# Padding a token tile, splitting the gather around a transpose, and re-laying the experts' weights in a hybrid GLA/GDN + MoE step on one Trainium2 core

## Chip, core and metric

The kernel runs on one NeuronCore of a Trainium2 chip. The metric is device time in microseconds, from the first to the last instruction of one launch. The engines are TensorE (PE, with its weight loads shown apart as PEld), VectorE (DVE), ScalarE (ACT), GpSimd (POOL) and SyncE (SP), which here issues all DMAs.

## What is computed

One decoder layer for 256 prompt tokens and 8 sequences of 4 sample tokens (288 tokens, width 1024): adaLN modulation, a mixer with a GLA and a Gated DeltaNet branch, an output projection, and then a hierarchical mixture of experts, which is the part that the change touches. All arithmetic is float32.

```python
def _moe(h, w_gr, b_gr, w_er, b_er, w_g, w_u, w_d):
    ...
    comb = ((one_hot(g_idx[:, 0], N_GROUPS) * g_w)[:, :, None] * within[:, None, :])
    for g in range(N_GROUPS):                       # 4 groups of 4 experts
        a = jnp.einsum('md,edf->mef', hf, w_g[g])   # D = 1024 -> F = 512
        u = jnp.einsum('md,edf->mef', hf, w_u[g])
        hid = jax.nn.silu(a) * u * comb[:, g, :, None]
        out = out + jnp.einsum('mef,efd->md', hid, w_d[g])
```

Each token goes to two of the sixteen experts (the top two of one group). An expert's three matrices are 1024 x 512, 1024 x 512 and 512 x 1024, 2 MB each.

## The kernel before

The program first runs the adaLN products, the input projections and the two mixer branches, with weights in a ring of five buffers (`W`, 1 MB each), then the output projection (`wout`), the second norm, the router, the experts, and the final norm. It is written by hand, one function per engine, with semaphores between engines.

**Router.** On PE, `token_major(m)` (L959) transposes the normed hidden state from feature-major (`hT`) to token-major, in three token tiles, `TILES = ((0, 128), (128, 128), (256, 32))`: two of 128 tokens and one of 32. ACT copies each half tile of 512 features from PSUM into `h2t` (L2211). DVE runs a chain of some forty small operations that picks groups and experts, and takes two exponentials from ACT on the way (L2221, L2224). POOL clears some tables and the accumulator `acc` (L2332 to L2337).

**Experts.** Eight blocks of two experts each. An expert has 64 token slots, a pair 128. DVE writes the one-hot matrix `Dg` (token x slot) of the pair and its weighted copy `Dc` in `dispatch` (L1815, L1818). The work of a block on PE (`expert_block`, L1004) is, in its order:

1. gate products, 16 matmuls (8 steps over the features, two experts, 64 output columns of the array each, 512 wide), into PSUM bank 2;
2. three transposes of `Dc` into bank 4 (L1025);
3. up products, 16 matmuls, into bank 3;
4. `gather` of the next block (L993): for each of 8 chunks of 128 features, three matmuls, one per token tile, that add up to the features of the 128 slots. The third one has a weight of 32 rows only, `h2t[0:32]`, since the last token tile has 32 tokens. Chunks 0 to 3 go to bank 0, 4 to 7 to bank 1;
5. four transposes of `hid` (L1035), after a wait for DVE, which makes `hid` = up x silu(gate) (L1843);
6. down products, 16 matmuls, after a wait for DVE, which copies the transposed `hid` from PSUM to `hidT` (L1847);
7. eight scatter products (L1050) of 288 columns each, which DVE adds to `acc` (L1854).

Each matmul in float32 is two passes on PE, so the profile counts 48 for the 24 matmuls of a gather. All of PE's products stand under the helper's line L431, transposes under L434. The gathered features of the next block are read by DVE (`gather_read`, L1827, bank 0) and ACT (L2229, bank 1). The last block has no gather. Blocks 0 to 5 are written as a loop of two, so that the gate weights of odd blocks lie in a buffer of their own (`gate2`). Experts with over 64 tokens would take a further loop (`overflow`, L474); in the profiled execution it ran no block.

**Weights.** SP loads a pair's gate, up and down weights, 4 MB each, with one DMA each (`load_expert`, L2427). Feature k x 128 + p goes to partition p, chunk k, so that each partition gets 16 runs of 2 KB for gate and for up, and 8 runs of 4 KB for down. The loads of a pair wait for PE's products of the pair before (L2449 to L2454): gate weights one block ahead (two buffers), up and down weights as soon as their one buffer is free.

Of the kernel before, what the change touches and what calls it, by code (L numbers as in the profile page):

```python
# [18 lines left out]
ALU = mybir.AluOpType  # L19
ACT = mybir.ActivationFunctionType  # L20
AX = mybir.AxisListType.X

P = 128
D = 1024
KD = D // P
# [3 lines left out]
TILES = ((0, 128), (128, 128), (256, 32))  # L29
# [28 lines left out]
PAIR = 2 * SLOTS  # L58
# [58 lines left out]
class Signals:  # L117
# [15 lines left out]
    def mark(self, kind, *events, by=1):  # L133
        sem = self.sem(kind)
        self.value[kind] += by
        for event in events:
            assert event not in self.marks, event
            self.marks[event] = (kind, self.value[kind])
        return sem

    def when(self, event):
        kind, value = ("first_building", 1) if self.counts is None else self.counts[event]
        return self.sem(kind), value
# [9 lines left out]
def _program(nc, ctx, I, O, known):  # L153
    S = Signals(nc, ctx, known)
    mark, when = S.mark, S.when
# [131 lines left out]
    h2t = carve(3, D)  # L287
    acc = carve(KD, TOK)
    Dg, Dc = carve(3, 2, SLOTS), carve(3, 2, SLOTS)
    DT_ = carve(TOK)  # L290
    hg = carve(KD, PAIR)
    hid = carve(DE)
# [24 lines left out]
    pm = [ctx.enter_context(nc.psum_tensor(f"bank{i}", [P, 512], F32)) for i in range(8)]  # L317

    T, V, A, G = nc.tensor, nc.vector, nc.scalar, nc.gpsimd
# [67 lines left out]
    for item in schedule:  # L387
        kind, c = item[0], item[-1]
# [38 lines left out]
    def rb(name):  # L427
        return pm[banks.get(name, 0)]
# [4 lines left out]
    def tr(out, in_, n):  # L433
        return T.transpose(out, in_, ident[0:n, 0:n])  # L434
# [53 lines left out]
    def _(pe):  # L488
# [501 lines left out]
            mm(b[0:q, 0:1], tri[0:q, 0:q], over[0:q, 0:1])  # L990
            mm(b[0:1, 8:9], over[0:q, 0:1], ones[0:q, 0:1]).then_inc(mark("router_products", "over ready"), 1)

        def gather(i, n):  # L993

            pe.wait_ge(n["dispatch"], i + 1)
            for g in range(2):
                for k in range(4):
                    for m, (o, w) in enumerate(TILES):
                        last = mm(pm[g][:, PAIR * k:PAIR * k + PAIR],
                                  h2t[0:w, m, 512 * g + 128 * k:512 * g + 128 * k + 128],  # L1000
                                  Dg[0:w, m].rearrange("p a b -> p (a b)"), m == 0, m == 2)
                last.then_inc(n["gathered"], 1)

        def expert_block(i, n, loaded_sem, second, gates, gates_loaded, more):  # L1004

            def products(out, lhs, kind, k, half, K):
                for x in range(2):
                    wt = (EW[:, kind] if kind else gates)[:, x * second, :].rearrange("p (k n) -> p k n", k=K)  # L1010
                    last = mm(out[SLOTS * x:SLOTS * x + SLOTS, :], lhs[:, k, SLOTS * x:SLOTS * x + SLOTS],
                              wt[:, k, 512 * half:512 * half + 512], k == 0, k == K - 1)
                return last

            pe.wait_ge(*gates_loaded)
            pe.wait_ge(n["gather_read0"], i + 1)
            for k in range(KD):
                if k == 4:
                    pe.wait_ge(n["gather_read1"], i + 1)
                last = products(pm[2], hg, 0, k, 0, KD)  # L1020
            last.then_inc(n["gate"], 1)

            pe.wait_ge(n["added"], KD * i + 1)
            for m, (o, w) in enumerate(TILES):
                last = tr(pm[4][0:PAIR, o:o + w], Dc[0:w, m].rearrange("p a b -> p (a b)"), w)  # L1025
            last.then_inc(n["scatter_matrix"], 1)
            pe.wait_ge(loaded_sem[1], 16 * (i + 1))
            for k in range(KD):
                last = products(pm[3], hg, 1, k, 0, KD)
            last.then_inc(n["up"], 1)  # L1030
            if more:
                gather(i + 1, n)
            pe.wait_ge(n["hidden"], i + 1)
            for f in range(4):
                last = tr(pm[5][:, PAIR * f:PAIR * f + PAIR], hid[0:PAIR, 128 * f:128 * f + 128], PAIR)  # L1035
            last.then_inc(n["turned"], 1)
            pe.wait_ge(loaded_sem[2], 16 * (i + 1))
            pe.wait_ge(n["turned_read"], i + 1)
            for g in range(2):
                for k in range(4):  # L1040
                    last = products(pm[6 + g], hidT, 2, k, g, 4)
                last.then_inc(n["down"], 1)
            pe.wait_ge(n["down_read0"], i + 1)
            for d in range(KD):

                if d == 3:
                    pe.wait_ge(n["down_read1"], i + 1)
                if d >= 4:
                    pe.wait_ge(n["added"], KD * i + d - 2)
                last = mm(pm[4 + d % 4][:, 0:TOK], yt[0:PAIR, 128 * d:128 * d + 128], DT_[0:PAIR, :])  # L1050
                last.then_inc(n["scattered"], 1)
# [44 lines left out]
    def _(dve):  # L1096
# [733 lines left out]
        def expert_block(i, n, next_dispatch):  # L1830

            s = sg2[0:PAIR]
            dve.wait_ge(n["softplus"], i + 1)
            V.scalar_tensor_tensor(s, pm[2][0:PAIR, :], 0.0, s, ALU.min, ALU.subtract).then_inc(n["log_sigmoid"], 1)  # L1834
            dve.wait_ge(n["scatter_matrix"], i + 1)
            V.tensor_copy(DT_[0:PAIR, :], pm[4][0:PAIR, 0:TOK]).then_inc(n["scatter_matrix_read"], 1)
            dve.wait_ge(n["sigmoid"], i + 1)
            V.tensor_tensor(s, pm[2][0:PAIR, :], s, ALU.mult).then_inc(n["silu"], 1)
            if next_dispatch:
                next_dispatch()  # L1840
            dve.wait_ge(n["silu"], i + 1)
            dve.wait_ge(n["up"], i + 1)
            V.tensor_tensor(hid[0:PAIR], pm[3][0:PAIR, :], s, ALU.mult).then_inc(n["hidden"], 1)  # L1843
            if next_dispatch:
                gather_read(i + 1, n)
            dve.wait_ge(n["turned"], i + 1)
            V.tensor_copy(hidT, pm[5][:, 0:4 * PAIR].rearrange("p (k s) -> p k s", s=PAIR)) \  # L1847
                .then_inc(n["turned_read"], 1)
            dve.wait_ge(n["down"], 2 * i + 1)
            V.tensor_copy(yt[0:PAIR, 0:512], pm[6][0:PAIR, :]).then_inc(n["down_read0"], 1)  # L1850
            dve.wait_ge(n["added"], KD * i + 1)
            for d in range(KD):
                dve.wait_ge(n["scattered"], KD * i + d + 1)
                V.tensor_tensor(acc[:, d, :], acc[:, d, :], pm[4 + d % 4][:, 0:TOK], ALU.add).then_inc(n["added"], 1)  # L1854
# [75 lines left out]
    def _(act):  # L1930
# [275 lines left out]
        def router():  # L2206
            def token_major(m):
                n = TILES[m][1]
                for g in range(2):
                    act.wait_ge(*when(f"h2t{m}{g} ready"))  # L2210
                    A.activation(h2t[0:n, m, 512 * g:512 * g + 512], rb(f"h2t{m}{g}")[0:n, :], ACT.Copy) \  # L2211
                        .then_inc(mark("router_by_scalar", f"read h2t{m}{g}"), 1)

            act.wait_ge(*when("router parts ready"))
            for i in range(4):
                act.wait_ge(*when(f"stored {chunk_of[('sgdn', i)]}"))
            A.activation(rparts, rb("router parts")[:, 0:TOK], ACT.Copy) \
                .then_inc(mark("router_by_scalar", "read router parts"), 1)
            token_major(0)
            act.wait_ge(*when("gd"))  # L2220
            A.activation(rs_["dd"], rs_["dd"], ACT.Exp).then_inc(mark("router_by_scalar", "gexp"), 1)  # L2221
            token_major(1)
            act.wait_ge(*when("ed"))
            A.activation(rs_["p1"], rs_["p1"], ACT.Exp).then_inc(mark("router_by_scalar", "eexp"), 1)  # L2224
            token_major(2)

        def gather_read(i, n):
# [49 lines left out]
    def _(pool):  # L2277
# [48 lines left out]
        def router():  # L2326

            pool.wait_ge(*when("merged 7"))
            pool.wait_ge(*when("wout7 ready"))
            for i in range(4):  # L2330
                pool.wait_ge(*when(f"stored {chunk_of[('sgdn', i)]}"))
            G.memset(rank, 0.0)  # L2332
            G.memset(comb, 0.0)
            G.memset(rt, 0.0).then_inc(mark("cleared", "rt zero"), 1)

            G.memset(acc, 0.0).then_inc(main_sems["added"], 1)
            G.memset(combJ, 0.0).then_inc(over_sems["added"], 1)  # L2337
# [5 lines left out]
    def _(sp):  # L2343
# [83 lines left out]
        def load_expert(kind, experts, n, sems, into=None):  # L2427

            sem = gate2_loaded if into is gate2 else sems[kind]
            into = EW[:, kind] if into is None else into  # L2430
            sp.dma_start(into[:, 0:n, :].rearrange("p a (k n) -> p (a k) n", k=4 if kind == 2 else KD),
                         wts[kind][experts].rearrange("a (k p) n -> p (a k) n", p=P)).then_inc(sem, 16)


        sp.wait_ge(*when("gdn2 oT1"))
# [87 lines left out]
```

## Time and profile before

| | before |
|---|---|
| median of 3 runs | 963.03 us (962.93 to 964.56) |
| profiled execution: its own time | 962.34 us |
| its span, first to last instruction | 960.4 us |
| PE busy | 876.6 us, 91% of the span |
| DVE, ACT, POOL busy | 399.9, 258.2, 35.2 us |
| moved by DMA | 190.65 MB, 199 GB/s over the span |
| expert blocks (first gather to the last scatter) | about 644 to 940 us |

The page gives shares of an average; the order of reading is: the forty slices for where the stages lie, the chain of work that ended last for what sets the end in a stage, then the timeline of one turn of the loop there. "PEclk" is the granted TensorE clock, 1.0 being 2.4 GHz and 0.5 being 1.2 GHz. A matmul's duration in the trace is its latency, so its rate is read from the starts of a stretch, not from the mean.

### The profile page before, as it was taken

How to read it: one execution, taken by the hardware profiler on the slowest of the kernel's cores; microseconds unless marked ns; L12 is line 12 of the kernel's file. 1: busy time of each engine (PE TensorE's matmuls, PEld its weight loads, DVE VectorE, ACT ScalarE, POOL GpSimd, SP SyncE). 2: the span in 40 equal slices, each digit the busy share in tenths (PEclk: the TensorE clock that was granted, in tenths of full speed). 3: DMA queues.
4: the chain of work that ended last, by engine and by line, in shares of the span. 5: the costliest groups of instructions: out<-in, count | busy, mean ns of one | idle time of the engine just before them, and what ended most of it. 6: DMA issues, size and time to landing. Idle time of an engine off the chain costs nothing.

```text
span 960.4 us, 12485 instructions
## 1 busy us (share of the span) xinstructions
PE 876.6 (91%) x4791; PEld 594.3 (62%) x4791; DVE 399.9 (42%) x992; ACT 258.2 (27%) x626; POOL 35.2 (4%) x84
## 2 busy tenths in 40 slices
PE   5889999898898899999999978779999999999995
PEld 3557777666666798879887736555544544544533
DVE  3120004656687855664555384341222222222216
ACT  3121103665554333434335320121011011011012
POOL 0000000000400000000001003000000000000000
PEclk9969999999998999999999957957999999999998
DMA  8947666522557321222216318991999998997621
GB/s 206 347 142 228 205 222 213 177 89 88 172 179 240 113 87 45 88 88 69 65 44 170 108 48 246 326 387 50 349 375 338 347 377 331 354 363 265 254 96 51
DMA packets 134412, 190.65 MB, mean 199 GB/s; under 512 B 6656, under 2 KB 90283, under 8 KB 134309
## 3 DMA queue, kind: packets, MB, share of 16 engines
q1 hardware_dynamic: 134360, 189.94, 58.7%
q8 instruction: 35, 0.57, 0.2%
q14 instruction: 17, 0.14, 0.1%
HBM read 178.98 MB, written 10.95 MB: 198 GB/s over the span
## 4 chain that ended last, share of the span: by engine, by line
PE 80%; DVE 10%; ACT 4%; issue 2%; SPq 2%; DMA 1%; DVEq 0%; POOL 0%; ACTq 0%; POOLq 0%
PE bank L431 78%; PE bank L434 3%; DVE arena L1693 2%; DMA arena<-in_w_ada 1%; DVE arena L1271 1%; DVE arena L1847 1%; DVE arena L1134 1%; ACT arena L1945 1%; SPq L2365 0%; ACT arena L1938 0%; DVE arena L1256 0%; ACT arena L1936 0%; ACT arena L1949 0%; DVE arena L1571 0%; ACT arena L2042 0%
## 5 line engine op out<-in xcount | busy, mean ns | idle before, releaser
L431 PE MATMUL bank<-arena 128*128 128x288 f32 (+8 forms) x4494 | 834.9, 414 | 60.4 <-DVE arena L1158 8.6
L431 PEld LDWEIGHTS bank<-arena 128*128 128x128 f32 (+4 forms) x4494 | 559.0, 174 | 322.2 <-issue 178.2
L434 PE MATMUL bank<-arena 128*128 128x128 f32 (+6 forms) x297 | 50.3, 302 | 18.7 <-DMA arena<-in_w_conv 7.3
L434 PEld LDWEIGHTS bank<-arena 128*128 128x128 f32 (+6 forms) x297 | 35.8, 154 | 38.9 <-issue 19.5
L2042 ACT ACTIVATE arena<-arena 128x288 f32<-128x288 f32 (+1 forms) x56 | 25.1, 448 | 122.0 <-DVE arena L1256 122.0
L1854 DVE TENSOR_TENSOR arena<-arena,bank 128x288 f32<-128x288 f32 x64 | 28.8, 455 | 29.4 <-PE bank L431 28.0
L1271 DVE SCALAR_TENSOR_TENSOR arena<-arena 128x312 f32<-128x312 f32 x72 | 39.4, 547 | 2.5
L1834 DVE SCALAR_TENSOR_TENSOR arena<-bank,arena 128x512 f32<-128x512 f32 x8 | 5.5, 692 | 77.2 <-ACT arena L2239 77.2
L1125 DVE TENSOR_TENSOR arena<-bank,arena 128x18 f32<-128x18 f32 x24 | 4.2, 174 | 77.9 <-PE bank L431 77.9
L2229 ACT ACTIVATE arena<-bank 128x512 f32<-128x512 f32 x8 | 4.8, 598 | 111.7 <-PE bank L431 111.7
L1940 ACT ACTIVATE arena<-arena 128x288 f32<-128x288 f32 (+4 forms) x60 | 33.5, 558 | 2.0
L2075 ACT ACTIVATE arena<-bank 128x288 f32<-128x288 f32 x40 | 16.2, 405 | 53.9 <-PE bank L431 30.2
L1256 DVE SCALAR_TENSOR_TENSOR arena<-arena 128x288 f32<-128x288 f32 (+1 forms) x56 | 25.9, 463 | 8.7 <-ACT arena L1940 8.7
L1434 DVE TENSOR_TENSOR arena<-arena 128x512 f32<-128x512 f32 x28 | 18.9, 690 | 23.0 <-PE bank L431 23.0
L1938 ACT ACTIVATE arena<-arena 128x288 f32<-128x288 f32 (+4 forms) x60 | 28.0, 466 | 1.9
L1504 DVE TENSOR_TENSOR arena<-arena,bank 128x512 f32<-128x512 f32 x24 | 16.5, 689 | 26.6 <-PE bank L431 26.6
L1936 ACT ACTIVATE arena<-arena 128x288 f32<-128x288 f32 (+2 forms) x57 | 25.5, 448 | 4.9 <-DMA arena<-in_cc 4.1
L2235 ACT ACTIVATE arena<-bank 128x512 f32<-128x512 f32 x8 | 4.8, 597 | 81.1 <-PE bank L431 81.1
L2245 ACT ACTIVATE arena<-bank 128x512 f32<-128x512 f32 x8 | 4.8, 598 | 71.0 <-PE bank L431 71.0
L1945 ACT ACTIVATE arena<-bank,arena 128x288 f32<-128x288 f32 x19 | 9.5, 500 | 48.7 <-PE bank L431 48.7
L1850 DVE COPY arena<-bank 128x512 f32<-128x512 f32 x8 | 5.5, 691 | 32.4 <-PE bank L431 32.4
L1827 DVE COPY arena<-bank 128x512 f32<-128x512 f32 x8 | 5.5, 692 | 31.1 <-PE bank L431 31.1
(238 smaller groups left out, 441.4 us busy)
## 6 DMA issues: line engine op xcount, KB each, us to landing
arena<-in_w_in SPq DMA_DIRECT2D x36, 1024.0 KB, 6.8
arena<-in_w_exp_gate SPq DMA_DIRECT2D x8, 4096.0 KB, 13.9
arena<-in_w_exp_up SPq DMA_DIRECT2D x8, 4096.0 KB, 17.1
arena<-in_w_exp_down SPq DMA_DIRECT2D x8, 4096.0 KB, 13.0
arena<-in_w_ada SPq DMA_DIRECT2D x24, 1024.0 KB, 5.6
arena<-in_state_gla SPq DMA_DIRECT2D x4, 1024.0 KB, 6.9
out_gla_s<-arena SPq DMA_DIRECT2D x4, 1024.0 KB, 8.9
arena<-in_w_out SPq DMA_DIRECT2D x4, 1024.0 KB, 6.1
```

The costliest lines, as they stand in the source:

```text
L431: return T.matmul(out, lhsT, rhs, start=start, stop=stop)
L434: return T.transpose(out, in_, ident[0:n, 0:n])
L1256: V.scalar_tensor_tensor(sg, y, 0.0, sg, ALU.min, ALU.subtract) \
L1271: V.scalar_tensor_tensor(y, x[:, j:j + YW], wv(j), y, ALU.mult, ALU.add) \
L1434: V.tensor_tensor(Lm[0:n, hs, 0:n], LT[0:n, hs, 0:n], mid(const(f"level{lv}")[0:n, 0:n], HG), ALU.mult) \
L1693: last = V.scalar_tensor_tensor(st, st, eSs[:, s, h:h + 1], pm[4 + j][:, P * q:P * q + P], ALU.mult, ALU.add)
L1854: V.tensor_tensor(acc[:, d, :], acc[:, d, :], pm[4 + d % 4][:, 0:TOK], ALU.add).then_inc(n["added"], 1)
L1936: A.activation(dst, src, ACT.Abs).then_inc(mark(kind, event + " abs"), 1)
L1938: A.activation(dst, dst, ACT.Exp, scale=-1.0).then_inc(mark(kind, event + " exp"), 1)
L1940: A.activation(dst, dst, ACT.Ln, bias=one[0:n]).then_inc(mark(kind, event), 1)
L1945: A.activation(dst, src, ACT.Ln, bias=const("eps")[0:n], scale=scale) \
L2042: A.activation(sg, sg, ACT.Exp).then_inc(mark("proj_by_scalar", f"sig{s3}"), 1)
```

## The change

Four edits. (a) The third token tile of `h2t` is cleared over all 128 partitions by POOL, ACT waits for that before it writes the 32 tokens, and the gather's third matmul takes 128 rows like the other two. (b) The gather of the next block is split: its first half (bank 0) stays where it was, its second half (bank 1) stands behind the four transposes of `hid`. (c) The weights of an expert are loaded so that partition p holds the features p x 8 + k (gate, up) and p x 4 + k (down), which lie side by side in memory: one run of 16 KB for each partition and expert. (d) To match, ACT writes `h2t` with its features permuted, with a step of 512 bytes between the elements it writes one after the other, and DVE makes `hid` from operands that it reads with a step of 16 bytes.

```diff
-        def gather(i, n):
+        def gather(i, n, halves=(0, 1)):
 
             pe.wait_ge(n["dispatch"], i + 1)
-            for g in range(2):
+            for g in halves:
                 for k in range(4):
-                    for m, (o, w) in enumerate(TILES):
+                    for m in range(3):
                         last = mm(pm[g][:, PAIR * k:PAIR * k + PAIR],
-                                  h2t[0:w, m, 512 * g + 128 * k:512 * g + 128 * k + 128],
-                                  Dg[0:w, m].rearrange("p a b -> p (a b)"), m == 0, m == 2)
+                                  h2t[:, m, 512 * g + 128 * k:512 * g + 128 * k + 128],
+                                  Dg[:, m].rearrange("p a b -> p (a b)"), m == 0, m == 2)
                 last.then_inc(n["gathered"], 1)
...
             if more:
-                gather(i + 1, n)
+                gather(i + 1, n, (0,))
             pe.wait_ge(n["hidden"], i + 1)
             for f in range(4):
                 last = tr(pm[5][:, PAIR * f:PAIR * f + PAIR], hid[0:PAIR, 128 * f:128 * f + 128], PAIR)
             last.then_inc(n["turned"], 1)
+            if more:
+                gather(i + 1, n, (1,))
...
-            V.tensor_tensor(hid[0:PAIR], pm[3][0:PAIR, :], s, ALU.mult).then_inc(n["hidden"], 1)
+
+            V.tensor_tensor(hid[0:PAIR].rearrange("s (k p) -> s k p", k=4),
+                            pm[3][0:PAIR, :].rearrange("s (p k) -> s k p", k=4),
+                            s.rearrange("s (p k) -> s k p", k=4), ALU.mult).then_inc(n["hidden"], 1)
...
-                    A.activation(h2t[0:n, m, 512 * g:512 * g + 512], rb(f"h2t{m}{g}")[0:n, :], ACT.Copy) \
+
+                    A.activation(h2t[0:n, m, :].rearrange("t (k c a) -> t c a k", k=KD, c=KD)[:, 4 * g:4 * g + 4],
+                                 rb(f"h2t{m}{g}")[0:n, :].rearrange("t (c a k) -> t c a k", c=4, k=KD), ACT.Copy) \
...
             A.activation(rs_["p1"], rs_["p1"], ACT.Exp).then_inc(mark("router_by_scalar", "eexp"), 1)
+            act.wait_ge(*when("h2t padding"))
             token_major(2)
...
             G.memset(rt, 0.0).then_inc(mark("cleared", "rt zero"), 1)
+            G.memset(h2t[:, 2, :], 0.0).then_inc(mark("cleared", "h2t padding"), 1)
...
-            sp.dma_start(into[:, 0:n, :].rearrange("p a (k n) -> p (a k) n", k=4 if kind == 2 else KD),
-                         wts[kind][experts].rearrange("a (k p) n -> p (a k) n", p=P)).then_inc(sem, 16)
+
+            sp.dma_start(into[:, 0:n, :], wts[kind][experts].rearrange("a (p k) n -> p a (k n)", p=P)) \
+                .then_inc(sem, 16)
```

On PE, in the loop of the experts, from the up products to the down products (the difference; in brackets the semaphores that an instruction waits for, `expert_hidden` being DVE's product L1843 and `expert_turned_read` its copy L1847):

```order
 L431 MATMUL bank<-arena 128x128 [waits expert_dispatch]
-L431 MATMUL bank<-arena 128x128 x23
+L431 MATMUL bank<-arena 128x128 x11
 L434 MATMUL bank<-arena 128x128 [waits expert_hidden]
 L434 MATMUL bank<-arena 128x128 x3
+L431 MATMUL bank<-arena 128x128 [waits expert_dispatch]
+L431 MATMUL bank<-arena 128x128 x11
 L431 MATMUL bank<-arena 64x512 [waits expert_turned_read,expert_loaded2]
```

Twelve of the gather's matmuls now stand between the transposes and the down products, which wait for DVE's copy.

On SP, the three loads of a pair in the loop, before and now (partitions x runs x elements):

```order
L2431 DMA arena<-in_w_exp_gate 128x16x512
L2431 ISA [waits expert_up]
L2431 DMA arena<-in_w_exp_up 128x16x512
L2431 DMA arena<-in_w_exp_down 128x8x1024 [waits expert_down]
```

```order
L2441 DMA arena<-in_w_exp_gate 128x2x4096
L2441 ISA [waits expert_up]
L2441 DMA arena<-in_w_exp_up 128x2x4096
L2441 DMA arena<-in_w_exp_down 128x2x4096 [waits expert_down]
```

Order and waits are the same; 16 or 8 runs in a partition have become 2 of 4096 elements.

## Rows read from the trace of the kernel before

**Rows 1.** The page, forty slices of 24 us: granted clock and DMA share, in tenths.
```profile
PEclk9969999999998999999999957957999999999998
DMA  8947666522557321222216318991999998997621
```

**Rows 2.** Chain that ended last, one loop turn, later the last block (start us, us, what).
```profile
719.42 0.70 DVE arena L1847
...
720.26 18.20 PE bank L431 x80
...
739.00 15.47 PE bank L431 x80
...
755.10 0.70 DVE arena L1847
...
924.52 0.70 DVE arena L1843
```

**Rows 3.** Timeline of that turn, weight loads (start us, us, [idle before <-releaser]).
```profile
745.96 8.32 PEld L431 LDWEIGHTS bank<-arena 128*128 128x128 f32 x48 [0.81 <-issue]
754.40 0.42 PEld L434 LDWEIGHTS bank<-arena 128*128 128x128 f32 x4
755.91 0.23 PEld L431 LDWEIGHTS bank<-arena 128*64 128x64 f32 x4 [1.08 <-issue]
```

**Rows 4.** Stretches, PEld alone: stretch, us, busy (count), clock, DMA share, GB/s.
```profile
745.96:754.40 8.44, 6.51 (x48) 1.00 1.03 386
497.89:503.25 5.36, 5.36 (x49) 1.00 0.00 0
```

**Rows 5.** Groups by form in the stretch 497.89 to 503.25 (count | busy us, mean ns).
```profile
L431 PEld LDWEIGHTS bank<-arena 128*128 128x128 f32 x49 | 5.6, 192 | 0.1
```

**Rows 6.** Timeline of that turn, VectorE, and SyncE's issue of the up weights.
```profile
746.15 0.69 DVE L1843 TENSOR_TENSOR arena<-bank,arena 128x512 f32<-128x512 f32 x1 [2.34 <-PE bank L431]
750.29 0.69 DVE L1827 COPY arena<-bank 128x512 f32<-128x512 f32 x1 [3.45 <-PE bank L431]
...
746.21 0.37 SPq L2431 DMA_DIRECT2D arena<-in_w_exp_up  x1
```

**Rows 7.** Stretches, PE alone: wout's start, first gather, first gate products.
```profile
579.95:586.00 6.05, 6.05 (x13) 0.50 0.71 210
586.00:618.00 32.00, 32.00 (x133) 1.00 0.86 282
644.00:658.97 14.97, 14.97 (x49) 0.50 0.27 99
658.97:661.09 2.12, 2.12 (x7) 0.50 0.00 0
```

**Rows 8.** Timeline of the router: ScalarE and VectorE.
```profile
631.92 1.07 ACT L2211 ACTIVATE arena<-bank 128x512 f32<-128x512 f32 x2
634.46 0.21 ACT L2224 ACTIVATE arena<-arena 128x12 f32<-128x12 f32 x1 [1.48 <-DVE arena L1778]
...
632.53 0.21 DVE L1775 TENSOR_TENSOR arena<-arena 128x48 f32<-128x48 f32 x1
632.77 0.23 DVE L1776 TENSOR_REDUCE arena<-arena 128x12 f32<-128x48 f32 x1
```

**Rows 9.** Timeline of the router: GpSimd's clearing of the accumulator.
```profile
614.79 2.02 POOL L2336 MEMSET arena<- 128x2304 f32 x1
```

**Rows 10.** Stretches, all engines: 4 KB runs, 2 KB runs, 12 KB runs among others.
```profile
731.00:738.00 7.00, 7.00 (x34) 2.18 (x32) 0.89 (x2) 0.00 (x0) 0.00 (x0) 1.00 1.02 412
741.00:762.00 21.00, 20.12 (x105) 10.85 (x103) 5.09 (x9) 1.23 (x2) 0.00 (x0) 1.00 1.03 385
...
8.00:11.00 3.00, 0.03 (x1) 0.03 (x1) 1.21 (x1) 1.69 (x3) 0.03 (x1) 1.00 1.21 237
```

**Rows 11.** DMA issues: KB each, median us to landing.
```profile
arena<-in_w_ada SPq DMA_DIRECT2D x24, 1024.0 KB, 5.6
...
arena<-in_const SPq DMA_DIRECT2D x1, 936.0 KB, 4.9
```

## Prediction

> **What bounds the kernel now.** I read the page first. Its slices show a granted clock of 1.0 nearly throughout the last third, and DMA busy to nine tenths there [rows 1]: the experts' stage could be bound by TensorE or by its weights. The chain of waits decides that. In the loop each turn takes 755.10 - 719.42 = 35.68 us, and all of it is PE but 0.70 us of VectorE's copy of the turned `hid` and its hand-over [rows 2]. No piece of the chain there is a DMA. So TensorE sets the pace, and only what shortens PE's own sequence counts. The timeline of the turn's weight loads then shows the two places that the edits touch: the gather's 48 passes, and the pause before the down products [rows 3].
>
> **Padding, edit (a).** The gather takes 754.40 - 745.96 = 8.44 us for 48 passes [rows 3, 4], 0.176 us each. The Gated DeltaNet branch has a stretch of passes with the same shape, all 128 rows high: 49 weight loads start within 5.36 us at the same clock [rows 4], 48 intervals of 0.1117 us. The present gather differs in its third matmul alone, 32 rows high, so that TensorE changes its tile size twice in each chunk. With all passes 128 high I take the stream's rate: 48 x 0.1117 = 5.36 us, which saves 3.08 us a turn. POOL's clearing of 1024 columns costs about 2.02 x 1024 / 2304 = 0.9 us [rows 9]. It starts at about 615 us, and its reader, ACT's third token tile, comes behind the exponential at 634.46 [rows 8], so it is hidden. If that cover were gone, 0.9 us would be added once.
>
> A rule speaks against this edit. The Trainium skill, TensorE: Matmul & The Clock Gate, Part 3 (The mechanism), says that a weight load overlaps running matmuls only where its row group differs from theirs. By that rule a column of full-height passes would hide no load and the padding would gain nothing. The trace disagrees: 49 loads of 192 ns each [rows 5] would need 9.4 us one after the other, and stood in 5.36 us.
>
> **Split, edit (b).** From the first load of the four transposes to that of the down products are now 755.91 - 754.40 = 1.51 us [rows 3], mostly the wait for DVE. With 12 matmuls behind the transposes, these cost four passes, 0.45 us, and PE goes on. For the change to 64-column tiles at the second half's end I add 0.10 us, an estimate between nothing and 0.19 us, what each of the 16 changes of tile size in a gather comes to (3.08 / 16). That saves 1.51 - 0.55 = 0.96 us a turn. The cover must hold: from the start of the gather's first half, at T = 0, the half lasts 2.7 us, DVE's product is ready at about 0.9 (it starts 0.2 after the last up product and takes 0.69) [rows 6], and the transposes end at 3.2. DVE reads the first half from 2.8 to 3.5, then copies the turned `hid` until about 4.3. PE reaches the down products at 5.9. So the wait has 1.6 us to spare, and the product 1.8 us.
>
> **Strided operands, edit (d).** DVE's product reads with a step of 16 bytes. The nearest row is a reduction that reads 48 elements with that step: 0.23 us against 0.21 for an operation on 48 contiguous ones [rows 8]. Scaled to 512 elements that is 0.2 us, upper bound twice its time, 0.7 us, lower bound nothing. In seven turns the 1.8 us cover it; in the last block, which has no gather, it lies in the chain [rows 2]. ACT's six copies to `h2t` write with a step of 512 bytes; no row shows such writes. The pair of 1.07 us has 1.48 us of slack before the second exponential [rows 8]. Up to 2.4 times their present time nothing moves; at four times the router's chain would be about 2 us late. I take nothing for both, since the nearest row shows almost nothing, and keep 0 to 2.7 us for the range.
>
> **Weights, edit (c).** Nothing waits for them now, so their layout is worth nothing by itself. But a turn shrinks to 35.68 - 3.08 - 0.96 = 31.64 us, and its three loads of 4.19 MB, 12.58 MB in that time, are 398 GB/s, where 2 KB runs moved 385 and 4 KB runs 412 GB/s while they streamed [rows 10]. Longer runs moved faster in every pair I can form: 1 MB in 1 KB runs landed 5.6 us after its issue, and 936 KB in runs of 7.5 KB 4.9 us after [rows 11]. I take 412 GB/s or more for runs of 16 KB, as the nearest row. Then the three loads of a turn take 30.5 us and keep up. What if they do not is rival B.
>
> **The first gather** is made at the low clock: 14.97 us, and the clock came up only 2.12 us into the gate products [rows 7]. A full-height pass at half the clock is twice 0.1117, so 48 take 10.7 us, a saving of 4.3. But it may also raise the clock earlier: wout's dense stream raised it 6.05 us after it began [rows 7], while today's gather, a third of whose passes change the tile size, did not in 14.97 us. I assume that it rises 5 us into the gather: 22.4 passes by then, the other 25.6 in 2.9 us, 7.9 us in all, a saving of 7.1; and the 2.12 us of gate products at half speed become 1.06. Together 8.1, with bounds of 4.3 (no rise before the gate products) and 9.1 (a rise after 3 us).
>
> **The sum.** Seven turns have a gather behind their up products: 7 x (3.08 + 0.96) = 28.3 us. With 8.1 for the first gather: 36.4 us. The profiled execution took 962.34 us, so 925.9; the median of the runs stands 0.7 above it, so 926.6 us. By the lower bound of the first gather and the upper ones of the strided operands it would be 933, by the best ends 924 to 925.
>
> **Rivals.**
> - **B, the weights become the bound.** Up weights have one buffer, so block 7's up load can only follow those before it. In the new schedule the first gate products start at 651.9, the first load of the loop is issued behind them at 658.9 and flows from about 661, and block 7 wants its up weights at 651.9 + 7 x 31.64 + 7.6 = 881. Nineteen loads of 4.19 MB lie in these 220 us, 79.7 MB: the bound begins below 362 GB/s, pauses included. Today's mean is 12.58 MB in 35.68 us, 353 GB/s, but with a pause in each turn, since loads wait for buffers. If 353 were all that the queue can give, block 7's up weights would come 226 - 220 = 6 us late and its down weights some 2.5 more: 935 us. For it: DMA share of nine tenths already [rows 1]. Against it: 385 and 412 GB/s while streaming [rows 10]. The Trainium skill, DMA: Bandwidth & Descriptors, Specifications, puts the limit of HBM for one core at about 358 GB/s; by that the loads would be 3 us late and the time 931 to 932. The trace disagrees already, with 412 GB/s over 7 us [rows 10].
> - **C, long runs are slow, and the kernel is slower than before.** One place has long runs: the convolution state, 24 partitions with 12 KB each, falls into a stretch that moved 237 GB/s [rows 10]. If 16 KB runs held the queue to 300 GB/s, the nineteen loads would take 266 us, 46 late, the last down load 5 more: 977 us. It decides below about 314 GB/s, where 34 us of lateness and some 2.5 of the last load eat the gain. Against it: that stretch is the program's start, with many small loads, and 24 partitions are few; the constants, 7.5 KB in all 128, were the quickest [rows 11].
> - **D, the padding gains nothing**, because a gather's pass waits for something else than its height, such as the alternation of weights. Then only the split is left, 7 x 0.96 = 6.7 us: 956.3. Against it: the stream at 0.1117 us also has a new weight for each pass, 49 loads [rows 4, 5]. The skill's rule cited under edit (a) would end here too.
>
> **How the numbers follow.** The forecast has 0.82: its terms come from rows of the same shape, and what is unsure is the first gather. B has 0.10, D 0.05, C 0.03. The range must leave out no more than 2 in 10: from 921, a little under the best ends, to 938, which takes in the strided operands and most of B. Left out are D, C, the rest of B and what is faster still, some 0.15. A measurement of this kernel can tell 0.2%, about 2 us, from no change. A, B and D are all faster by more: 0.96 with a rest for the unforeseen; C gives slower, 0.03, and 0.01 is left for no change.
>
> **What would show it.** In the profile after, the turn of the loop should be 31.6 us; the gather's two halves 2.7 us each, with no idle PE before the down products; the clock at 1.0 before the first gather ends; the first gate products at about 652 us. If PE waits in the loop for `in_w_exp_up`, it is B or C, and the loads' time to landing tells which. If the halves still take 4.2 us each, it is D. If VectorE's product takes over 2.5 us, the split's cover is gone and the transposes wait. The prediction is wrong if the turn is above 33 us, or if the router's chain has grown by over 3 us.

## Result and profile after

| | before | changed |
|---|---|---|
| median of the runs made side by side | 962.98 us (961.65 to 964.56) | 924.14 us (922.52 to 924.96) |
| ratio | | 0.9594, 95% interval 0.9574 to 0.9614 |
| profiled execution: time, span | 962.34, 960.4 us | 924.96, 923.1 us |

The change is 4.1% faster; forecast were 926.6 us, in a range from 921 to 938. In the profiled executions the difference is 962.34 - 924.96 = 37.4 us, of a sum of 36.4 forecast.

The page's forty slices after the change, granted clock and DMA share, answer to [rows 1]:

```profile
span 923.1 us, 12487 instructions
...
PEclk9969999999999899999999995896999999999998
DMA  8955765543267711233111632797499999997711
```

The slices of the last third look as before; what changed shows in the chain. The chain of work that ended last, one turn of the loop, the first piece of the next, then the last block (start us, us, what), answers to [rows 2]:

```profile
668.25 20.79 PE bank L431 x104
689.04 0.55 PE bank L434 x3
689.58 9.91 PE bank L431 x56
699.49 0.44 PE bank L434 x4
699.93 20.81 PE bank L431 x104
...
886.88 1.06 DVE arena L1846
...
888.68 0.70 DVE arena L1852
```

A turn is 699.93 - 668.25 = 31.68 us, and VectorE has left it: the piece of 104 passes runs from the gather's second half through the down and scatter products into the next gate products without a break. Only the last block, which has no gather, still waits for VectorE twice, and the product there has grown from 0.70 [rows 2] to 1.06 us.

The timeline of TensorE's weight loads in one turn (start us, us, [idle before <-releaser]) answers to [rows 3]:

```profile
728.24 2.75 PEld L431 LDWEIGHTS bank<-arena 128*128 128x128 f32 x24 [0.81 <-issue]
730.92 0.47 PEld L434 LDWEIGHTS bank<-arena 128*128 128x128 f32 x4
731.36 3.08 PEld L431 LDWEIGHTS bank<-arena 128*128 128x128 f32 x28
```

The first half starts at 728.24 and the transposes at 730.92: 2.68 us for 24 passes, 0.1117 each, which is the rate of the Gated DeltaNet stream [rows 4] to the digit. The second half follows the transposes by 0.44 us; its row of 28 runs on into the first four loads of the down products. Before, the down products followed the transposes by 1.51 us [rows 3], most of it a wait.

Stretches of the changed kernel: of all engines, with stretch, us, then busy time and count of PE, PEld, DVE, ACT and POOL, granted clock, DMA share and GB/s. The first two lie in the first gather, the third is one turn, the fourth a load of down weights, the last nearly the whole loop:

```profile
644.00:647.50 3.50, 3.50 (x19) 3.50 (x18) 0.00 (x0) 0.00 (x0) 0.00 (x0) 0.50 0.00 0
647.50:651.00 3.50, 3.50 (x28) 2.97 (x29) 0.69 (x1) 0.60 (x1) 0.00 (x0) 0.97 0.00 0
700.00:731.00 31.00, 31.00 (x163) 15.00 (x162) 8.96 (x17) 3.78 (x6) 0.00 (x0) 1.00 0.97 395
734.00:741.00 7.00, 7.00 (x35) 2.30 (x34) 0.69 (x1) 0.60 (x1) 0.00 (x0) 1.00 1.01 433
662.00:840.00 178.00, 178.00 (x948) 90.33 (x945) 53.42 (x96) 20.07 (x32) 0.00 (x0) 1.00 0.97 398
```

The clock rises inside the first gather, at about 647.7 us, 5.6 us after it began at 642.1; before, it stayed at half through all of it [rows 7]. In the loop PE is busy for 178 us of 178, at the full clock, while the queue moves 398 GB/s at a share of 0.97.

Timelines of VectorE, ScalarE and GpSimd (start us, us, [idle before <-releaser]): the product that makes `hid`, the copies to `h2t`, the second exponential, and the clearing of the padded tile, answer to [rows 6, 8]:

```profile
728.43 1.07 DVE L1846 TENSOR_TENSOR arena<-bank,arena 128x512 f32<-128x512 f32 x1 [2.34 <-PE bank L431]
...
629.88 1.89 ACT L2217 ACTIVATE arena<-bank 128x512 f32<-128x512 f32 x2
...
632.43 0.21 ACT L2231 ACTIVATE arena<-arena 128x12 f32<-128x12 f32 x1 [0.66 <-DVE arena L1780]
...
612.97 0.95 POOL L2343 MEMSET arena<- 128x1024 f32 x1
```

Strides cost something after all: the product takes 1.07 us where it took 0.69, and a pair of overlapping copies 1.89 where it took 1.07 [rows 8]. Both are covered: the product's 1.07 us lie under a half gather of 2.68, and ScalarE's slack before the exponential shrinks from 1.48 to 0.66 us but does not end. VectorE's chain of the router, from L1740 to the last weight, takes 8.40 us in both traces.

### The profile page after: what moved, and what is told of

It is laid out like the page before. It is cut to its first block, busy times and chain, and to the rows that moved or that the text cites. A ratio compares the mean times of both kernels' runs of the same rounds, so it can differ in the third digit from the quotient of the medians.

```text
span 923.1 us, 12487 instructions
## 1 busy us (share of the span) xinstructions
PE 843.6 (91%) x4791; PEld 578.1 (63%) x4791; DVE 402.5 (44%) x992; ACT 260.6 (28%) x626; POOL 36.1 (4%) x85
## 4 chain that ended last, share of the span: by engine, by line
PE 80%; DVE 10%; ACT 4%; issue 2%; SPq 2%; DMA 1%; POOL 0%; DVEq 0%; ACTq 0%; POOLq 0%
PE bank L431 78%; PE bank L434 3%; DVE arena L1695 2%; DMA arena<-in_w_ada 1%; DVE arena L1273 1%; DVE arena L1136 1%; ACT arena L1950 1%; SPq L2374 1%; POOL arena L2331 0%; ACT arena L1943 0%; DVE arena L1258 0%; ACT arena L1941 0%; ACT arena L1954 0%; DVE arena L1573 0%; DVE arena L1468 0%
## 5 line engine op out<-in xcount | busy, mean ns | idle before, releaser
L431 PE MATMUL bank<-arena 128*128 128x288 f32 (+8 forms) x4494 | 806.0, 409 | 55.7 <-DVE arena L1160 8.6
L431 PEld LDWEIGHTS bank<-arena 128*128 128x128 f32 (+4 forms) x4494 | 544.5, 174 | 301.8 <-issue 168.5
L434 PE MATMUL bank<-arena 128*128 128x128 f32 (+6 forms) x297 | 48.0, 291 | 19.2 <-DMA arena<-in_w_conv 7.6
L1855 DVE COPY arena<-bank 128x512 f32<-128x512 f32 x8 | 5.5, 691 | 43.5 <-PE bank L431 43.5
L1982 ACT ACTIVATE arena<-arena 128x288 f32<-128x288 f32 x8 | 3.5, 443 | 50.9 <-DVE arena L1731 50.9
```

The lines of the kernel that those rows point to most:

```text
L431: return T.matmul(out, lhsT, rhs, start=start, stop=stop)
```

## Experiments

Line numbers are those of each kernel. The median of before differs a little between comparisons, so ratios are given.

**Padding alone (`pad_only`).** Edit (a) without the others.

```diff
-                    for m, (o, w) in enumerate(TILES):
+                    for m in range(3):
...
-                                  h2t[0:w, m, 512 * g + 128 * k:512 * g + 128 * k + 128],
-                                  Dg[0:w, m].rearrange("p a b -> p (a b)"), m == 0, m == 2)
+                                  h2t[:, m, 512 * g + 128 * k:512 * g + 128 * k + 128],
+                                  Dg[:, m].rearrange("p a b -> p (a b)"), m == 0, m == 2)
...
+            act.wait_ge(*when("h2t padding"))
...
+            G.memset(h2t[:, 2, :], 0.0).then_inc(mark("cleared", "h2t padding"), 1)
```

> Edit (a) alone on the kernel before. Theory (a pass of the gather costs 0.112 us once all passes are 128 rows high, because the tile size no longer changes): the gather falls from 8.44 to 5.4 us, the turn from 35.68 to 32.6 us, the first gather and its gate products save about 7.7 us: 963.0 - 7 x 3.08 - 7.7 = 933.7 us. Rival (the padding gains nothing without the other edits, or the weights at 2 and 4 KB runs hold up a turn under 35 us): 945 to 963 us, with PE waiting for the weights.

Measured: 928.88 us (928.18 to 930.46), ratio 0.9656, interval 0.9638 to 0.9673. The chain, one turn:

```profile
703.17 0.70 DVE arena L1847
704.01 18.20 PE bank L431 x80
...
722.76 12.59 PE bank L431 x80
735.35 0.45 PE bank L434 x4
735.82 0.70 DVE arena L1847
```

The turn is 735.82 - 703.17 = 32.65 us, 3.03 less than 35.68, as forecast; 2.88 of it lie in the piece with the gather (15.47 to 12.59), the rest in the transposes behind it (0.60 to 0.45). The first gather and gate products, one piece of 84 passes, went from 24.07 to 16.41 us in the chain, 7.7 less. Seven turns and this piece make 28.9; the whole is 33.4 us in the spans (960.4 to 927.0). Of the other 4.5 us, 2.5 lie ahead of the first gather (its piece starts at 640.52 us instead of 643.03) and 0.3 behind the last scatter, in code that the edit does not touch. The last 1.7 lie in the down and scatter products of the last block, whose code is the same too, before and here:

```profile
926.80 12.88 PE bank L431 x48
895.38 11.18 PE bank L431 x48
```

The granted clock made that difference: 0.57 in the first 3.7 us of this piece before (926.80 to 930.50), 1.00 in the same place here (895.38 to 898.90). The changed kernel's trace has 12.88 us there too, so these 1.7 us are no part of its gain.

**Split alone (`split_only`).** Edit (b) without the others.

```diff
-                gather(i + 1, n)
+                gather(i + 1, n, (0,))
...
+            if more:
+                gather(i + 1, n, (1,))
```

> Edit (b) alone. Theory (PE's pause before the down products is the wait for VectorE's copy, and half a gather covers it): 0.96 us a turn in seven turns, 956.3 us; the first gather as before, 15.0 us. Rival (the pause is the change of tile size at the start of the down products, not the wait): nothing, 963 us.

Measured: 948.9 us (945.83 to 953.18), ratio 0.9855, interval 0.983 to 0.988. The chain:

```profile
700.38 11.26 PE bank L431 x56
711.63 0.59 PE bank L434 x4
712.22 22.15 PE bank L431 x104
...
746.17 0.59 PE bank L434 x4
746.76 22.14 PE bank L431 x104
```

The turn is 746.76 - 712.22 = 34.54 us: 1.14 less, where 0.96 were forecast. Together the two edits save 4.00 in a turn, so behind the padding the split is worth 32.65 - 31.68 = 0.97, as forecast. That it is worth 0.17 more alone, about one change of tile size, agrees with the order of passes: there the gather's last change, out of a 32-row tile, also leads to the 64-column tiles of the down products, which in the padded gather are a change more. This is argued from the order and was not tried by itself. Seven turns make 8 us. Between the profiled spans are 9.1 (960.4 to 951.3), but stretches outside the loop enter into that with up to 3 us either way: the first gather's piece starts 3.1 us earlier and takes 1.3 longer (25.36 against 24.07). The median is 14 below that of before, among runs that spread over 7 us. What goes beyond the loop's 8 us is not shown to be the split's.

**Layout alone (`runs_only`).** Edits (c) and (d) without the others.

```diff
-            V.tensor_tensor(hid[0:PAIR], pm[3][0:PAIR, :], s, ALU.mult).then_inc(n["hidden"], 1)
+            V.tensor_tensor(hid[0:PAIR].rearrange("s (k p) -> s k p", k=4),
+                            pm[3][0:PAIR, :].rearrange("s (p k) -> s k p", k=4),
+                            s.rearrange("s (p k) -> s k p", k=4), ALU.mult).then_inc(n["hidden"], 1)
...
-                    A.activation(h2t[0:n, m, 512 * g:512 * g + 512], rb(f"h2t{m}{g}")[0:n, :], ACT.Copy) \
+                    A.activation(h2t[0:n, m, :].rearrange("t (k c a) -> t c a k", k=KD, c=KD)[:, 4 * g:4 * g + 4],
+                                 rb(f"h2t{m}{g}")[0:n, :].rearrange("t (c a k) -> t c a k", c=4, k=KD), ACT.Copy) \
...
-            sp.dma_start(into[:, 0:n, :].rearrange("p a (k n) -> p (a k) n", k=4 if kind == 2 else KD),
-                         wts[kind][experts].rearrange("a (k p) n -> p (a k) n", p=P)).then_inc(sem, 16)
+            sp.dma_start(into[:, 0:n, :], wts[kind][experts].rearrange("a (p k) n -> p a (k n)", p=P)) \
+                .then_inc(sem, 16)
```

> Edits (c) and (d) alone: 16 KB runs and the permuted features. Theory (no piece of the chain waits for weights): 963.4 us, the 0.4 us being VectorE's strided product in the last block. Rival (the layout itself carries part of the gain): 955 us or less.

Measured: 962.35 us (956.28 to 964.51), ratio 1.0003, interval 0.998 to 1.0026: nothing, as forecast. The turn says it with less noise: at the full clock it takes 35.66 to 35.69 us, as before, and two turns lost time to the clock (last section).

**The changed kernel without its layout (`short_runs`).** Edits (a) and (b), with the diffs shown under `pad_only` and `split_only`; weights in the old runs of 2 and 4 KB, no strided operand.

> Edits (a) and (b) without (c) and (d): the weights in runs of 2 and 4 KB as before. Theory (the queue still gives the 362 GB/s that the single buffers of up and down need, pauses included): no wait for weights, 924.1 - 0.4 = 923.7 us, the same as the changed kernel within 1 us. Rival (the shorter turn outruns 2 KB runs, so that (c) is what lets the other edits pay): late up weights in the last blocks, 929 to 937 us.

Measured: 923.17 us (919.28 to 925.32), ratio 0.9583, interval 0.9558 to 0.9607, the same as the changed kernel's. Its turn is 31.69 us (701.40 to 733.09 in the chain), where the changed kernel has 31.68. So the layout gives nothing at the new pace either. How near it is to mattering shows in the stretch of nearly the whole loop, which in the changed kernel is the last row of the stretches above:

```profile
662.00:840.00 178.00, 178.00 (x950) 89.68 (x947) 50.93 (x95) 20.37 (x33) 0.00 (x0) 1.00 1.03 392
```

A turn asks for 12.58 MB in 31.68 us, 397 GB/s. The short runs give 392 with all DMA engines busy throughout (share 1.03, before it was 353 with pauses): they fall behind by some 1%, and the loads' lead takes that up. The long runs move what is asked with pauses left (0.97), and 433 GB/s while they stream.

**Shorter runs (`runs_1k`, `runs_512`).** To find from where the weights bound the loop, `short_runs` with its loads cut into column pieces: 1 KB runs (2 DMAs for gate and up each, 4 for down) and 512 B runs (4 and 8); `parts` is the number of DMAs that PE's waits count. The diff of `runs_1k` against `short_runs`:

```diff
-            sp.dma_start(into[:, 0:n, :].rearrange("p a (k n) -> p (a k) n", k=4 if kind == 2 else KD),
-                         wts[kind][experts].rearrange("a (k p) n -> p (a k) n", p=P)).then_inc(sem, 16)
+            K = 4 if kind == 2 else KD
+            dst = into[:, 0:n, :].rearrange("p a (k n) -> p (a k) n", k=K)
+            src = wts[kind][experts].rearrange("a (k p) n -> p (a k) n", p=P)
+            width = 1024 if kind == 2 else 512
+            step = width if n == 1 else 256
+            for c0 in range(0, width, step):
+                sp.dma_start(dst[:, :, c0:c0 + step], src[:, :, c0:c0 + step]).then_inc(sem, 16)
...
-            pe.wait_ge(loaded_sem[1], 16 * (i + 1))
+            pe.wait_ge(loaded_sem[1], 16 * parts[0] * (i + 1))
```

> Edits (a) and (b), with the weights in runs of 1 KB, each load in two or four DMAs by columns. Theory (bound by the weights below 362 GB/s, single buffers for up and down): 1 KB runs streamed at 347 GB/s at the start of the program before; nineteen loads take 230 us instead of 220, the last up weights come 10 us late and the last down weights 3 more: 923.2 + 12 = 935 us, PE waiting for the weights in the last blocks alone. Rival (the slack of the buffers holds, as with 2 KB runs): 923 us.

> The same with runs of 512 bytes, each load in four or eight DMAs. Theory: at about 300 GB/s nineteen loads take 266 us, 46 late, the last down load 5 more: 973 us, slower than the kernel before; turns of some 42 us from the third block on. Rival (it degrades by less since the first turns run on loads that are already in): 940 to 955 us.

Measured: 1 KB 942.18 us (937.03 to 943.41), ratio 0.9785, interval 0.9743 to 0.9826; 512 B 983.67 us, ratio 1.0229, interval 1.0181 to 1.0278. The same stretch, 1 KB:

```profile
662.00:840.00 178.00, 167.54 (x878) 83.44 (x875) 46.60 (x88) 18.87 (x30) 0.00 (x0) 0.98 1.09 348
```

and 512 B:

```profile
662.00:840.00 178.00, 146.46 (x745) 72.02 (x745) 39.80 (x75) 16.31 (x26) 0.00 (x0) 0.92 1.19 289
```

The waits of TensorE between 640 and 920 us, 1 KB (us in total, times, longest):

```profile
PE bank L431 <- DMA arena<-in_w_exp_up: 14.9, 5, 4.4
```

and the chain there:

```profile
847.62 17.97 DMA arena<-in_w_exp_up
865.63 11.66 PE bank L431 x56
```

So rival B, and with 512 B rival C, are what happens when the loads are slow enough: PE stands before the up products, and with 512 B for 1.3 us twice before down products. (Both versions also issue two to eight DMAs where one stood, so run length and number of DMAs are not told apart; for the bound only the rate counts.) Both runs were later than expected, by 7 and 11 us, and the chain of the 1 KB version shows why. There the last wait for up weights is that of block 6, at 865.63 us, not of block 7. Seventeen loads, 71.3 MB, lie before it, and at 348 GB/s they take 204.9 us: from 660.7 to 865.6, without a pause. Block 7 only adds a down and an up load, 24 us at this rate, to a turn that has no next gate load. So the point at which weights begin to bound is 71.3 MB over the time until block 6 wants its up weights: with the prediction's own times 651.9 + 6 x 31.64 + 7.6 - 661 = 188.3 us, 379 GB/s. By this, 348 GB/s are 16.6 us late and 289 are 58.4; measured against `short_runs` are 19.0 and 60.5. The 2 us that are left go with a lower clock: 0.98 and 0.92 in these stretches, and 0.64 from 757 to 761 us, just after a wait of 4.4 us in the 1 KB version. How much the clock cost was not tried by itself.

**Half the tile-size changes (`paired_tiles`).** The kernel before, no padding: in odd chunks the 32-row tile goes first, so that two such tiles stand side by side and 8 changes of tile size are left of 16. The rows and the work stay the same.

```diff
-                    for m, (o, w) in enumerate(TILES):
+                    for at, m in enumerate((2, 0, 1) if k % 2 else (0, 1, 2)):
+                        w = TILES[m][1]
...
-                                  Dg[0:w, m].rearrange("p a b -> p (a b)"), m == 0, m == 2)
+                                  Dg[0:w, m].rearrange("p a b -> p (a b)"), at == 0, at == 2)
```

> The kernel before, with the last tile still 32 rows high, but taken first in every odd chunk, so that two 32-row matmuls stand side by side and a gather changes its tile size 8 times, not 16. Theory (each change costs 3.08 / 16 = 0.19 us): the gather 8.44 - 1.54 = 6.9 us, the turn 34.1 us, with about 2 us of the first gather 950 us. Rival (a 32-row pass is slow in itself, or the accumulation over three tiles is): gather 8.44 us, turn 35.7 us, 962.5 us.

Measured: 947.74 us (943.51 to 948.33), ratio 0.9842, interval 0.9804 to 0.9881. The timeline of weight loads in one turn:

```profile
740.96 6.97 PEld L431 LDWEIGHTS bank<-arena 128*128 128x128 f32 x48 [0.81 <-issue]
747.85 0.47 PEld L434 LDWEIGHTS bank<-arena 128*128 128x128 f32 x4
```

The gather takes 6.89 us; it was 8.44 with 16 changes [rows 3] and is 5.36 with none. Half the changes cost half the excess: 0.19 us each at the full clock. It is the change of size that costs, not the short tile: its 16 short passes are all still there. This is what the padding removes, shown without padding.

**A step further (`dc_moved`, `changed_again`, `dc_again`).** A turn still has the three transposes of `Dc` between gate and up products, one of them 32 rows high. In `dc_moved`, which is `short_runs` otherwise, they stand behind the scatter products of the block before.

```diff
+        def scatter_matrix(n):
+            for m, (o, w) in enumerate(TILES):
+                last = tr(pm[4][0:PAIR, o:o + w], Dc[0:w, m].rearrange("p a b -> p (a b)"), w)
+            last.then_inc(n["scatter_matrix"], 1)
...
-            pe.wait_ge(n["added"], KD * i + 1)
-            for m, (o, w) in enumerate(TILES):
-                last = tr(pm[4][0:PAIR, o:o + w], Dc[0:w, m].rearrange("p a b -> p (a b)"), w)
-            last.then_inc(n["scatter_matrix"], 1)
+            if over:
+                pe.wait_ge(n["added"], KD * i + 1)
+                scatter_matrix(n)
...
+            if more:
+                pe.wait_ge(n["added"], KD * i + 6)
+                scatter_matrix(n)
...
+            pe.wait_ge(main_sems["added"], 1)
+            scatter_matrix(main_sems)
```

> Edits (a) and (b) with short runs, and the three transposes of Dc moved from between the gate and up products (64-column tiles) to behind the scatter products of the block before (128-column tiles, as they are). Theory (PE's changes of tile size cost 0.1 to 0.2 us each wherever they stand): two changes fewer in a turn, 31.68 - 0.3 = 31.4 us, 923.2 - 2.4 = 920.8 us. Rival (changes between the forms of full height cost nothing, or PE waits for VectorE's adds in the new place): turn of 31.7 us or more, 923 to 926 us.

Measured: 919.3 us (914.82 to 924.68), ratio 0.9553, interval 0.9514 to 0.9592. The chain, one turn:

```profile
698.64 13.78 PE bank L431 x72
712.42 0.39 PE bank L434 x3
712.81 16.80 PE bank L431 x88
729.60 0.44 PE bank L434 x4
730.04 13.77 PE bank L431 x72
```

The turn is 730.04 - 698.64 = 31.40 us, 0.28 less, with two changes of tile size fewer. Since the ranges of this version and of the changed kernel overlapped in separate comparisons, both ran side by side once more.

> The changed kernel beside the version with the moved transposes, on one chip. Both theories: 924 us, turn 31.68 us, 0.37 us of VectorE's strided product in the last block.

> The version with short runs and the transposes of Dc behind the scatter products. Theory (its turn of 31.40 us against 31.68 counts, and so does the contiguous product in the last block): 7 x 0.28 + 0.37 = 2.3 us below the changed kernel of the same comparison, 921.7 us, and in more than half of the pairs of runs. Rival (the stretches outside the loop, which vary with the granted clock by several us from run to run, hide it): the medians lie within 1 us of each other.

Measured: the changed kernel 924.91 us (923.28 to 927.53), this version 919.92 us (915.06 to 924.76), and lower in each of the six rounds, by 0.5 to 11.6 us. It is the fastest version here. Of the 6.0 us between the two profiled spans (925.7 and 919.7) 3.2 lie ahead of the first gather, where the two don't differ, and 2.6 between the first gather's start and the last scatter (904.92 - 643.52 = 261.40 against 899.17 - 640.35 = 258.82); 2.3 were expected there. That much is shown; how much of the rest belongs to the version stays open.

## Why the prediction was right, point by point

- **What bounds.** PE's own sequence did: the turn shrank by 4.00 us, the padding's and the split's terms, and `runs_only` gave nothing.
- **Padding**, 3.08 us a turn forecast: 3.03 alone. The rate of the full-height stream was the right row, and `paired_tiles` shows that the cause named, the change of tile size, is the cause. Rival D, at 956.3 us, fell with the halves at 2.68 us. The rule of the Trainium skill, TensorE: Matmul & The Clock Gate, Part 3 (The mechanism), that loads overlap only when the row group differs, fell with it: 24 loads of one row group started within 2.68 us. That a load recorded with 0.19 us [rows 5] can overlap the next load's record does not yet show it hidden behind a matmul; a second stream does. At the full clock the output projection's passes, 288 columns wide and 128 rows high with a new weight each, take 32.00 / 133 = 0.241 us [rows 7], those of 128 columns 0.112. If the columns cost alike, 160 of them take 0.129 us and 128 take 0.103, so by this estimate a new weight adds about 0.01 us to a pass.
- **Split**, 0.96 forecast: 0.97 behind the padding. Of the 1.51 us, 0.97 are saved and 0.44 still go to the transposes, which leaves 0.10 for the change to 64 columns, as estimated.
- **First gather and gate products**, 8.1 forecast. The gather took 8.15 us (642.10 to 650.25) instead of 14.97, 6.8 less; from the first gate to the first up products were 7.58 us instead of 8.60, 1.0 less: 7.8. The rise of the clock was assumed 5 us into the gather, and came 5.6 into it. It was not this one trace's luck: gather and gate products, one piece of the chain, took 16.34 to 16.55 us in five traces with the padding and the transposes of `Dc` in place (`after`, `pad_only`, `short_runs`, `runs_1k`, `changed_again`), and 24.07 to 25.36 in the three with 16 changes in a gather (`before`, `split_only`, `runs_only`).
- **Strided operands**, nothing forecast, up to 2.7 allowed. VectorE's product grew by 0.38 us, which shows in the last block alone, 0.36 in the chain; ScalarE's copies grew from 0.58 to 1.05 us (medians of six), 1.8 times as long where 2.4 times were free. The value taken, nothing, was too low by these 0.36 us; the prediction's own scaling of its row gave 0.2 us, from a reduction of 48 elements in SBUF.
- **The sum.** 7 x 4.00 + 7.8 - 0.36 = 35.4 us, between the first gather and the last scatter (295.7 us before, 260.3 now); 36.4 were forecast there. The other 2.0 us of the 37.4 lie ahead of the first gather (it started at 644.0, now at 642.1) in code that is the same, and are no merit of the change: the piece of the first gather, which starts at 641.0 us in this trace of the changed kernel, starts at 643.5 in its trace `changed_again` and at 643.0 in that of before. So the mechanism missed by 1.0 us, and luck of 2.0 turned that into a total 1.0 us better than forecast in the profiled executions.
- **Weights, and the rivals B and C.** They kept up. The landing times (KB each, median us), before and then changed, bear on the question whether long runs are slow:

```profile
arena<-in_w_exp_gate SPq DMA_DIRECT2D x8, 4096.0 KB, 13.9
arena<-in_w_exp_up SPq DMA_DIRECT2D x8, 4096.0 KB, 17.1
arena<-in_w_exp_down SPq DMA_DIRECT2D x8, 4096.0 KB, 13.0
...
arena<-in_w_exp_gate SPq DMA_DIRECT2D x8, 4096.0 KB, 13.8
arena<-in_w_exp_up SPq DMA_DIRECT2D x8, 4096.0 KB, 16.1
arena<-in_w_exp_down SPq DMA_DIRECT2D x8, 4096.0 KB, 14.4
```

  They don't settle it: down loads landed later than before, and a landing time counts what is left of the load ahead (the first up load of the loop was issued 7.55 us after the gate load, at 665.12 us). The rate does: long runs were not slow, with 433 GB/s while streaming where 412 or more were taken. The limit of about 358 GB/s in the Trainium skill, DMA: Bandwidth & Descriptors, Specifications, did not hold in this program on one core: 398 GB/s over the whole loop. One step failed, the threshold of B, "the bound begins below 362 GB/s": it took block 7, which has no next gate load ahead of it, where block 6 decides, at 379. At the 353 GB/s of rival B the 71.3 MB take 202.0 us, so the loads would have been 13.7 us late, and the time about 940 rather than 935. It did not touch the result, since even the short runs gave 392, but their margin was 3% and not 8%.
- **What would have been a fair doubt** is the value of edits (c) and (d): the prediction carried them as a need of the new pace, and `short_runs` shows that the pace is reached without them.

## What to carry to other kernels

Look for a small tile in an otherwise uniform column of matmuls: its passes may be cheap while the two changes of size around it are not, and padding with zeros, or pairing the small tiles, removes them. A stage on TensorE that ends in a wait for another engine can be filled with half of a neighbour's work, if that half has no reader in a hurry. Before a new layout is built for a transfer, work out the rate that the new pace asks for, at the block that decides (here the last but one), and try the pace without the layout.

## What was not expected of the hardware

- A change between tiles of 128 and 32 rows costs TensorE 0.19 us at the full clock, nearly two passes of 0.1117 us.
- By run length, the loads of 4 MB moved 289 GB/s in 512 B, 348 in 1 KB (both cut into two to eight DMAs), 392 in 2 and 4 KB runs, and 398 in 16 KB runs, where the last were not the limit (433 while streaming).
- VectorE read 512 elements of PSUM and of SBUF with a step of 16 bytes in 1.07 us instead of 0.69, and ScalarE wrote 512 with a step of 512 bytes in 1.05 instead of 0.58 (medians of six).
- The granted clock can fall inside the loop. In `runs_only` two of the seven turns took 37.4 us instead of 35.67, and the stretches behind their pause, 0.87 us without work on PE behind the four transposes, show it, at 0.57:

```profile
718.50:722.50 4.00, 3.86 (x10) 1.41 (x12) 0.00 (x0) 0.00 (x0) 0.00 (x0) 0.57 0.97 410
756.00:760.00 4.00, 3.98 (x12) 1.52 (x14) 0.00 (x0) 0.00 (x0) 0.00 (x0) 0.57 0.97 414
```

  The kernel before has the same sequence on PE there and stayed at 1.0 in its profiled execution, as did every other loop here in which PE did not wait for weights. The last block, where PE waits for VectorE twice, shows the same outside the loop: its down and scatter products took 12.88 us in the traces of `before`, `after`, `changed_again` and `dc_again`, at 0.51 to 0.58 in their first 3.4 to 3.7 us, and 11.18 in the eight others. What decides it is open.
- The times of one kernel go with the granted clock of the run: `dc_moved` took 914.8 us at a mean clock of 0.954 and 924.7 at 0.942, so that differences under 5 us need the chain, not the total.
